# Moving the kept-state product of the HGRN2 scan from ScalarE to GpSimd, and the diagonals to the end of VectorE's round

## The reference

```
def step(S, inp):
    qc, kc, vc, gc = inp
    b = jnp.cumsum(gc, axis=2)
    o = jnp.einsum('bhtd,bhde->bhte', qc * jnp.exp(b), S)
    rel = jnp.exp(jnp.where(causal, b[:, :, :, None, :] - b[:, :, None, :, :], -jnp.inf))
    att = jnp.einsum('bhtd,bhsd,bhtsd->bhts', qc, kc, rel)
    o = o + jnp.einsum('bhts,bhse->bhte', att, vc)
    b_end = b[:, :, -1:, :]
    S = (S * jnp.exp(b_end[:, :, 0, :, None])
         + jnp.einsum('bhsd,bhse->bhde', kc * jnp.exp(b_end - b), vc))
    return S, o
```

## Time and profile before

| | us |
|---|---|
| median of 3 runs | 3042.78 |
| lowest and highest | 3037.58, 3047.19 |
| the profiled execution, its own time | 3047.19 |
| its span, first to last instruction | 3045.4 |
| PE, DVE, ACT, POOL busy over the span | 2654.7, 884.6, 548.9, 218.2 |
| the scan stage, first GpSimd clear to the last output copy | 2132.32 to 2242.66 |

### The profile page before, as it was taken

How to read it: one execution, slowest core, us unless ns; L and a number is a source line. 1 busy time by engine, 2 the same in 40 slices (tenths; PEclk the granted TensorE clock), 3 DMA queues, 4 the chain that set the end, 5 groups by cost and what they waited for, 6 DMA issues and landing times. The chain is left out here.

```text
span 3045.4 us, 44485 instructions
## 1 busy us (share of the span) xinstructions
PE 2654.7 (87%) x18608; PEld 1421.0 (47%) x18608; DVE 884.6 (29%) x1598; ACT 548.9 (18%) x892; POOL 218.2 (7%) x209
## 2 busy tenths in 40 slices
PE   5798996989887695999999969999669869999993
PEld 2243442888885253444443434444544534444441
DVE  6233001666565534111110122000762431101013
ACT  3342000223233311000000011300451100000000
POOL 0000000001010400001010000000010010100100
PEclk9999998999998897999999989999889979999997
DMA  3242133131323523799999940221433259999995
GB/s 117 112 143 99 62 103 97 45 82 48 82 49 151 212 118 140 259 413 410 411 407 399 392 152 38 94 79 55 118 130 136 95 196 377 417 413 417 413 404 225
DMA packets 264767, 617.51 MB, mean 203 GB/s; under 512 B 37377, under 2 KB 128658, under 8 KB 262546
## 3 DMA queue, kind: packets, MB, share of 16 engines
q1 hardware_dynamic: 233362, 524.72, 46.3%
q10 hardware_dynamic: 17408, 56.63, 4.7%
q0 software_dynamic: 13824, 33.58, 2.8%
HBM read 545.67 MB, written 85.98 MB: 207 GB/s over the span
## 5 line engine op out<-in xcount | busy, mean ns | idle before, releaser
L1812 PE MATMUL moe_first_psum<-moe_ring,moe_first_x_t 128*64 128x512 f32 (+1 forms) x1504 | 508.9, 599 | 7.3 <-DMA moe_ring<-in_moe_w_in 3.7
L560 PE MATMUL proj_psum<-proj_mix,proj_ring 128*128 128x512 f32 x768 | 337.1, 599 | 15.9 <-ACTq L72 10.1
L1812 PEld LDWEIGHTS moe_first_psum<-moe_ring,moe_first_x_t 128*64 128x64 f32 (+1 forms) x1504 | 198.1, 165 | 280.0 <-issue 275.2
L1812 PE MATMUL moe_first_psum<-moe_ring,moe_first_act_t 128*128 128x512 f32 (+1 forms) x800 | 282.1, 594 | 0.0
L1408 PE MATMUL moe_route_psum<-moe_ring,trunk_mixed 128*128 128x512 f32 x512 | 230.3, 605 | 22.8 <-PEq L106 22.8
L560 PEld LDWEIGHTS proj_psum<-proj_mix,proj_ring 128*128 128x128 f32 x768 | 147.1, 193 | 200.4 <-issue 188.7
L1853 DVE TENSOR_TENSOR moe_first_act<-moe_first_silu,moe_first_psum 128x512 f32<-128x512 f32 x48 | 33.0, 688 | 688.6 <-ACT moe_first_silu L1869 688.6
L2146 PE MATMUL hproj_psum<-trunk_mixed,moe_ring 128*128 128x512 f32 x512 | 220.0, 592 | 1.8 <-ACTq L72 1.8
L1812 PE MATMUL moe_first_psum<-trunk_mixed,moe_first_x_t 128*128 128x512 f32 (+1 forms) x544 | 196.1, 593 | 0.0
L1812 PEld LDWEIGHTS moe_first_psum<-moe_ring,moe_first_act_t 128*128 128x128 f32 (+1 forms) x800 | 105.8, 162 | 131.5 <-issue 131.5
L1408 PEld LDWEIGHTS moe_route_psum<-moe_ring,trunk_mixed 128*128 128x128 f32 x512 | 96.9, 194 | 137.2 <-issue 137.2
(11 more groups left out here) (339 smaller groups left out, 3075.2 us busy)
## 6 DMA issues: line engine op xcount, KB each, us to landing
moe_ring<-in_moe_w_in SPq DMA_DIRECT2D x94, 2048.0 KB, 18.0
moe_ring<-in_moe_w_out SPq DMA_DIRECT2D x50, 2048.0 KB, 19.9
trunk_mixed<-in_moe_w_in SPq DMA_DIRECT2D x34, 2048.0 KB, 20.3
trunk_mixed<-in_moe_w_out SPq DMA_DIRECT2D x14, 2048.0 KB, 21.1
moe_ring<-expert_rows SPq DMA_DIRECT2D x16, 1024.0 KB, 7.9
proj_ring<-in_rw_in SPq DMA_DIRECT2D x12, 1024.0 KB, 6.1
moe_ring<-gate_cm SPq DMA_DIRECT2D x16, 512.0 KB, 4.4
normed_rows<-moe_x SPq DMA_DIRECT2D x16, 512.0 KB, 2.6
```

The source lines that it names most:

```text
L560: mm = pe.matmul(psum[:, bank + half, :], ring[slot][:, k, part * P:(part + 1) * P], src[:, k, half * HALF:(half + 1) * HALF], start=(k == ...
L1812: mm = t.matmul(e.psum[rows, bank + a, :], left[:, k0 + k, rows], weights.units[m % RING][:, k, a * HALF:(a + 1) * HALF], start=(part != " ...
```

## The change

GpSimd gets the product `kept = state * e_end`, as one `tensor_tensor` of 128 x 512 for each chunk, behind the same two waits as before (the previous state, and `e_end` of the span). `between` is a semaphore that is increased between the waits and that nobody waits for. ScalarE loses `keep_state` and the wait on `ready` at its start. In VectorE's round the `diagonals` of chunk c + 2 move from the front to a place behind `state_mid` of chunk c + 1, ahead of `decays`.

```
         def _(g):
             for z in (*q_bd, *k_bd, state, state_mid[0]):
                 g.memset(z[:], 0.0).then_inc(zeroed, 1)
             g.wait_ge(zeroed, 8)
             g.sem_inc(ready, 1)
+            pool.open(g)
+
+            def chunk_part(chunk, i, quad):
+                g.wait_ge(dve.sem, dve.after("S", chunk - 1))
+                g.sem_inc(between, 1)
+                if i % 2 == 0:
+                    g.wait_ge(a_span.sem, a_span.after("end", (quad * 2 if quad is not None else last_quad * 2) + i // 2))
+                    g.sem_inc(between, 1)
+                g.tensor_tensor(kept[:], state[:], of_chunk(e_end, chunk), ALU.mult).then_inc(pool.sem, 1)
+
+            all_quads(g, chunk_part)
...
         # VectorE
             def chunk_part(chunk, i, quad):
                 b = i % 2
                 q2 = last_quad * 2 if quad is None else quad * 2
-                if has(2, i, quad):
-                    diagonals(chunk + 2, (i + 2) % 4, q2 + (i + 2) // 2)
                 if has(1, i, quad):
                     causal(chunk + 1, 1 - b)
                 v.wait_ge(pe.sem, pe.after("S", chunk))
                 v.tensor_tensor(grown[:], bank(6 + b), of_chunk(e_late, chunk), ALU.mult).then_inc(dve.sem, 1)
                 v.wait_ge(dve.sem, dve.after("grown", chunk))
-                v.wait_ge(keep.sem, keep.after("kept", chunk))
+                v.wait_ge(pool.sem, pool.after("kept", chunk))
                 v.tensor_add(state[:], kept[:], grown[:]).then_inc(dve.sem, 1)
                 if has(1, i, quad):
                     v.wait_ge(dve.sem, dve.after("S", chunk))
                     v.wait_ge(pe.sem, pe.after("o", chunk - 1))
                     v.tensor_tensor(state_mid[1 - b][:], state[:], of_chunk(e_mid, chunk + 1), ALU.mult).then_inc(dve.sem, 1)
+                if has(2, i, quad):
+                    diagonals(chunk + 2, (i + 2) % 4, q2 + (i + 2) // 2)
                 if quad is not None and b == 0:
                     decays(q2 + i // 2 + 2, 2, 48 * (SPANS - 2))
...
         # ScalarE
-            def keep_state(chunk, i, quad):
-                a.wait_ge(dve.sem, dve.after("S", chunk - 1))
-                if i % 2 == 0:
-                    a.wait_ge(a_span.sem, a_span.after("end", (quad * 2 if quad is not None else last_quad * 2) + i // 2))
-                for m in range(HG_PAIRS):
-                    mul = a.activation(kept[:, m, :], state[:, m, :], ACT.Copy,
-                                       scale=e_end[:, ds(chunk, 1), m:m + 1].rearrange("p n m -> p (n m)"))
-                mul.then_inc(keep.sem, 1)
...
             def chunk_part(chunk, i, quad):
-                keep_state(chunk, i, quad)
                 if has(1, i, quad):
                     rows(chunk + 1, 1 - i % 2)
...
-            a.wait_ge(ready, 1)
             decays(0)
```

More of the change, by code:

```diff
@@ L2289, in hgrn_scan @@
         arrived = [s.sem(f"arrived{n}") for n in range(3)]
-        ready, zeroed = s.sem("ready"), s.sem("zeroed")
+        ready, zeroed, between = s.sem("ready"), s.sem("zeroed"), s.sem("between")
         v_in = [s.sem(f"v_in{b}") for b in range(2)]
@@ L2300, in hgrn_scan @@
         dve = s.progress("dve", ["grown", "S", "mid"], credit=2)
-        keep = s.progress("keep", ["kept"], credit=2)
+        pool = s.progress("pool", ["kept"], credit=2)
         block = s.block()
@@ L2429, in _ @@
             act.open(a)
[L2430 to L2439, removed]
             def decays(span):
```

## The result

The changed kernel takes 3082.49 us in the median of 4 runs (3077.12 to 3084.77), the kernel before 3043.98 in the runs beside it. By these medians it is slower by 38.5 us, where 41 were forecast. The ratio is 1.012, 95% interval 1.0104 to 1.0137, which is 32 to 42 us: small, but clear of the noise. The span of its profiled execution is 3078.9 us.

What follows compares the result with a forecast made beforehand. VectorE's instruction stream was taken to bound the scan, whose time passes directly into the kernel's. 28 us of waits for TensorE plus 13 us of holds by GpSimd made 41 us on 3042.78: 3084 us, range 3066 to 3096.

Steps and rivals of the forecast that it cites:

- Step 4: Scan, diagonals moved behind `state_mid`: VectorE must wait for TensorE's results from the late `k_bd`; 28 us.
- the last chunk: End of the scan: after the last waiting `grown` (chunk 14) TensorE works as before; 0.
- One sign: Expected in the profile: `grown` waits two or more microseconds for TensorE in each round without `decays` before it.
- The prices inside step 4: Per wait without `decays`: 2.0 us at full clock, 3.6 at half; with `decays`: 0 or 1.1 us.
- The share of two thirds: TensorE's clock low part of the time: 16 us at full clock plus 2/3 of 18.3 makes 28 us.
- The argument for the clock: TensorE pauses 2.6 us or more each round, longer than the 2.10 us that were enough, so its clock falls in most rounds.
- Step 3: VectorE behind `state_mid`: GpSimd's product holds the first diagonal, 1.0 us in each of 13 rounds; 13 us.
- Step 2: GpSimd's `kept` product, 1.19 us, is ready at least 3.8 us before `state` needs it; as a wait 0.
- Step 1: ScalarE loses four activations per chunk, but isn't the bound and VectorE doesn't wait for it; 0.
- GpSimd's product didn't slip into the stalls: Rival: GpSimd's product hides in VectorE's stalls, its hold costing 0; + 28 us, 3071; chance 0.14.
- the clock was neither high nor low throughout: Rivals: TensorE's clock high throughout, 29 us, 3072, chance 0.12; or low throughout, 48 to 50 us, 3092, chance 0.12.
- not slower: Rival: the chain from `state` over `state_mid` to TensorE paces the scan; earlier `state_mid` gives 3041, at most 3036; chance 0.04.

Runs made afterwards that it cites:

- e8: Kernel before, with `state_mid` made by ScalarE in four activations, and `kept` also ahead of ScalarE's exponentials; ratio 0.9983, scan 75.23 us (before: 80.86).
- e9: Kernel before, with both `state_mid` on ScalarE and `state` fused into four instructions without `grown`; ratio 0.9973, median 3030.97 us, scan 72.44 us.
- e5: Kernel before, with VectorE's `grown` and `state` replaced by four `scalar_tensor_tensor` of 128x128 from PSUM and `kept`; ratio 0.999, scan 81.40 us.
- e6: Changed kernel, with TensorE's product "S" of a chunk queued ahead of the next chunk's attention products and transposes; ratio to before 1.0081, scan 105.79 us.
- e7: Kernel before with only the diagonals moved behind `state_mid`, and ScalarE making the next chunk's `kept` ahead of its exponentials; ratio 1.0065, scan 101.51 us.
- e10: Changed kernel, with 10 result-neutral products of a constant block added on TensorE behind its output products; ratio to before 1.0089, scan 110.29 us.
- e2: Kernel before with only `kept` moved to GpSimd, the diagonals staying at the front of VectorE's round; ratio 1.0035, scan 90.50 us.
- e11: Kernel before with only `kept` on GpSimd, which also waits for `k_bd` so it runs beside `causal` and `grown`; ratio 1.0001, scan 80.70 us.
- e4: Changed kernel, with GpSimd also waiting for TensorE's attention product of the next chunk before making `kept`; ratio to before 1.0087, scan 108.11 us.
- e1: Kernel before with only the diagonals moved behind `state_mid`, `kept` left on ScalarE in its old order; ratio 1.0123, scan 115.55 us.
- e3: Changed kernel, with 20 result-neutral products of a constant block added on TensorE behind its output products; ratio to before 1.0107, scan 119.03 us.

## Why the prediction was right, point by point

- The bound and the place were right: VectorE's stream paces the scan, and the scan's loss is the kernel's. e8 and e9 show it from the other side: work taken off VectorE shortens the scan. But only 5.6 us of e8's 9.4 us less busy time, and nothing in e5, came out as time, so another limit lies close behind.
- Step 4, the diagonals behind `state_mid`: right in mechanism, shown by e6 (the queue) and e7 (the order alone). 28 us were forecast, 26.9 measured. The waits stand in the rounds that I named; the entry for `grown` counts also the last chunk, 1.31 us (0.6 before), which I had at 0. One sign was drawn wrongly: I expected `grown` to wait two or more microseconds in each of these rounds. `causal`, which stands first, took 1.25 to 2.25 us of each wait and left `grown` 0.64 to 1.87.
- The prices inside step 4. At full clock 2.0 us for a round was right (1.89 to 2.09 in e10). At half clock 3.6 us was too low: the one round of the changed kernel that ran slowly from `ahead` to the end of "S" cost 2.25 + 1.87 = 4.12. The row that I took for the half clock, with 1.74 us for eight products, lay in part at full clock; eight that lie wholly at half clock take 2.07 and 1.92.
- The share of two thirds: 26.9 - 16 = 10.9 us were added by the clock, of 18.3 in my reckoning, which looks near. With the measured half-clock price the full span is about 25 us (an estimate: 8 x (4.12 - 2.0) for the rounds without `decays`, and 5 x 1.6 in place of 5 x 1.1 for the others), and 10.9 is some 0.4 of it. So the share was too high and the price too low, and that 28 came out so close is in part luck.
- The argument for the clock was weak as well. I took a pause of over 2.10 us as enough to make TensorE slow. In the changed kernel itself three pauses of 3.14 to 3.27 us between 2174 and 2209 have full speed behind them, and one of 2.61 us has half speed. In e7 there were eleven pauses of 1.28 to 3.00 us with products at full speed behind them, and one of 1.85 us with products at half speed (1.86 us for eight). The length of the last pause alone does not say it. That the half clock costs these microseconds is shown by e10; what makes it fall in one round and not in another stays open.
- Step 3, the hold by GpSimd: right in mechanism (e2, e11), 13 times as forecast, but 0.85 us each instead of 1.0: 11.0 us instead of 13. The product of the row that I took is a longer one: 1.19 us, where the product here takes 1.04 with nothing in its way (e11). In both places the hold is some 0.2 us less than the product alone: 0.975 of 1.19, 0.85 of 1.04.
- The rule of the Trainium skill ("SBUF — State Buffer", Who interferes with whom), an exclusive lock for the whole instruction, agrees in kind: the two `q_bd` products that are held end at 2181.22, so with their usual 0.85 us they began at about 2180.37, close to the 2180.51 at which GpSimd's record ends. As a price the whole product was an upper bound that isn't reached. The list of what can be held on the same page of the Trainium skill has `tensor_scalar` too, in a two-port mode; e4's clamp of 1.15 instead of 0.43 us fits it, though no row shows the mode.
- What steps 3 and 4 had as a plain sum isn't one: against e7 the move to GpSimd costs 18.1 us and not 11.0, since the waits grow with it.
- Step 2: right, `state` never waits for GpSimd.
- Step 1, ScalarE's relief at 0: right as a term against the kernel before. But with the new order `kept` on ScalarE comes late, 9.6 us (e1), so against e1 GpSimd's move nearly pays for its own hold. Another order on ScalarE takes all but 0.3 us of these waits away without GpSimd (e7). I had not seen this when I wrote what e1 should bring, and took the two halves for additive: alone they cost 34.7 and 9.6 us, 44.3 in sum, together 38.7.
- The rivals: GpSimd's product didn't slip into the stalls; the clock was neither high nor low throughout; "not slower" fell with the first wait of `grown`.

## What to carry to other kernels

In a stage of hand-ordered streams, count for each wait how much work of the waiting engine lies between the operand that it hands over and the result that it needs back, and read the other engine's queue in order: here a product that was long ready to run stood behind one that was not. Work moved to GpSimd is free or dear by what VectorE does beside it: the same product cost 9.6 us behind `state_mid`, where products with two SBUF inputs follow (e2), and nothing beside `causal` and `grown`, which have one input in PSUM (e11). When an order changes, ask again of each engine that was "off the path" whether its cover is still there, and test one half of a change only with that repaired.

## What the runs showed of the hardware

- A GpSimd product of 128x512 took 1.04 us beside VectorE instructions with one SBUF input and one in PSUM (e11), and 1.30 to 1.48 us where it began during a VectorE product with two SBUF inputs (the changed kernel, e2), 1.53 in e4. GpSimd got its turn between back-to-back VectorE instructions.
- The VectorE instruction behind was longer by the time from its own start to the end of GpSimd's record, less 0.14 us: 0.98 and 0.84 (2179.53 in the changed kernel), 0.79 and 0.65 (e2, where it came later), 0.86 and 0.72 (e4's clamp), 1.11 and 0.975.
- A VectorE `tensor_scalar` from SBUF to SBUF (0.43 us) is held as well: 1.15 us (e4).
- A `scalar_tensor_tensor` of 128x128 out of PSUM steps at 0.27 us. Four of them with the round trip to `state_mid` took 1.27 us (e5), three quarters of the 1.66 us of the two instructions of 128x512 that they replace.
- Ten added products in each pause kept TensorE's granted clock over the scan at 0.97 (0.87 without them) and made the stage shorter, by 9.3 us (e10). Twenty kept it at 0.99 and gained 0.6 us, since they stood in the way (e3).
